# Feed-forward stages: each row product of 512 columns issued as two products of 256 columns

## What is computed

```
a = relu(h @ w1) ** 2        # w1: 1024 x 4096, a: 256 x 4096
x = x + gate * (a @ w2)      # w2: 4096 x 1024
```

## Time and profile before

| | us |
|---|---|
| Median of three executions | 1924.4 |
| Lowest and highest of them | 1923.17, 1924.47 |
| Span of the profiled execution, first to last instruction | 1914.2 |
| Median time minus that span | 10.2 |
| TensorE busy (share of span) | 1775.9 (93%) |
| VectorE busy | 779.1 (41%) |
| ScalarE busy | 490.0 (26%) |

### The profile page before, as it was taken

One profiled execution on the slowest core, in us unless ns is written; L12 is line 12 of the kernel. 1 busy time (PEld: TensorE's weight loads), 2 busy tenths in 40 slices (PEclk: granted clock), 3 DMA queues, 4 the chain that ended last, 5 costly groups with the idle time before them and its releaser, 6 DMA issues. The chain is left out here.

```text
span 1914.2 us, 23879 instructions
## 1 busy us (share of the span) xinstructions
PE 1775.9 (93%) x9783; PEld 1091.0 (57%) x9784; DVE 779.1 (41%) x1062; ACT 490.0 (26%) x593; POOL 72.3 (4%) x89
## 2 busy tenths in 40 slices
PE   6998889999999998999889898799899999989999
PEld 5873664333333333333323332598799977668898
DVE  5647661222112212212112121567754566666544
ACT  4334421001001000001000000443434453445442
POOL 7300000000000000000000000200000000000000
PEclk9999889999999999999999999899999999989999
DMA  8649799999999999999999999653365544775551
GB/s 291 219 136 385 264 421 398 427 428 428 427 427 427 428 427 427 428 427 427 428 428 427 428 427 419 226 193 124 133 220 176 176 147 163 266 262 178 193 182 63
DMA packets 133859, 598.28 MB, mean 313 GB/s; under 512 B 16897, under 2 KB 17041, under 8 KB 109057
## 3 DMA queue, kind: packets, MB, share of 16 engines
q1 hardware_dynamic: 126160, 589.34, 77.8%
q10 hardware_dynamic: 6800, 5.38, 1.0%
q0 software_dynamic: 800, 2.11, 0.3%
HBM read 595.70 MB, written 1.11 MB: 312 GB/s over the span
## 5 line engine op out<-in xcount | busy, mean ns | idle before, releaser
L175 DVE TENSOR_TENSOR wl<-raw,wh 128x2048 fp32r<-128x2048 f32 x126 | 289.5, 2328 | 85.4 <-ACT wh L169 85.3
L169 ACT ACTIVATE wh<-raw 128x2048 fp32r<-128x2048 f32 x126 | 236.6, 1912 | 171.0 <-PE banks L204 106.1
L1420 DVE COPY hid<-banks 128x512 f32<-128x512 f32 x32 | 22.1, 692 | 520.2 <-PE banks L1371 520.2
L233 PE MATMUL banks<-xth,wh 128*128 128x256 f32 x800 | 224.3, 280 | 8.0 <-DVE xtl L304 3.3
L233 PE MATMUL banks<-xtl,wh 128*128 128x256 f32 x800 | 223.4, 279 | 0.0
L233 PE MATMUL banks<-xth,wl 128*128 128x256 f32 x800 | 223.2, 279 | 0.0
L1371 PE MATMUL banks<-moe_halves,xs 128*64 128x512 f32 x816 | 187.4, 604 | 8.3 <-DMA moe_halves<-in_w_exp_in 8.3
L233 PEld LDWEIGHTS banks<-xth,wh 128*128 128x128 f32 x800 | 151.2, 189 | 9.6 <-DVE xtl L304 3.7
L233 PEld LDWEIGHTS banks<-xth,wl 128*128 128x128 f32 x800 | 151.3, 189 | 0.0
L233 PEld LDWEIGHTS banks<-xtl,wh 128*128 128x128 f32 x800 | 150.9, 189 | 0.3
L204 PE MATMUL banks<-wh,xth 128*128 128x512 f32 x320 | 128.8, 402 | 7.2 <-DVE wl L175 3.3
(11 more groups left out here) (409 smaller groups left out, 2250.4 us busy)
## 6 DMA issues: line engine op xcount, KB each, us to landing
moe_halves<-in_w_exp_in SPq DMA_DIRECT2D x51, 2048.0 KB, 40.9
raw<-in_mlp_w SPq DMA_DIRECT2D x64, 1024.0 KB, 5.6
moe_left<-in_w_exp_in SPq DMA_DIRECT2D x26, 2048.0 KB, 34.9
moe_halves<-in_w_exp_out SPq DMA_DIRECT2D x25, 2048.0 KB, 43.4
raw<-in_w_exp_in SPq DMA_DIRECT2D x25, 2048.0 KB, 40.0
raw<-in_ada_w SPq DMA_DIRECT2D x48, 1024.0 KB, 7.9
moe_left<-in_w_exp_out SPq DMA_DIRECT2D x14, 2048.0 KB, 43.1
moe_gates<-in_w_exp_in SPq DMA_DIRECT2D x13, 2048.0 KB, 38.7
```

The source lines that it names most:

```text
L169: act.activation(c.wh[:, slot], c.raw[:, slot], ACT.Copy).then_inc(c.high_ready, 1)
L175: dve.tensor_tensor(c.wl[:, slot], c.raw[:, slot], c.wh[:, slot].bitcast(F32), ALU.subtract).then_inc(c.low_ready, 1)
L233: mm = pe.matmul(out, w[:, slot, k, cols], x[:, k0 + k, :], start=first and k == 0 and j == 0 and b % 2 == 0, stop=last and k == CK - 1 an ...
L1420: dve.tensor_copy(c.hid[:, 1, :], c.bank[hid_banks(c, par) + 1]).then_inc(it.up_kept, 1)
```

## The change

A new function `multiply_halves` takes the place of `multiply_rows` in the feed-forward stages, for every row chunk but the last of the last quarter (which stays with `multiply_last`). Each product of 512 columns is issued as two of 256 columns, into the first and the second half of the same bank, with the same stationary operand, which the program loads again for the second half. The start flag is set for the first half alone.

```diff
+def multiply_halves(c, pe, n, slot, k0, banks, first, last, xh, xl):
+
+    pe.wait_ge(c.low_ready, n + 1)
+    for k in range(CK):
+        for m in range(len(banks)):
+            toks = slice(m * P, m * P + P)
+            for j, (x, w) in enumerate(((xh, c.wh), (xh, c.wl), (xl, c.wh))):
+                for b in range(2):
+                    cols = slice(b * COLS // 2, b * COLS // 2 + COLS // 2)
+                    mm = pe.matmul(banks[m][:, cols], x[:, k0 + k, toks], w[:, slot, k, cols],
+                                   start=first and k == 0 and j == 0 and b == 0, stop=last and k == CK - 1 and j == 2,
+                                   skip_group_check=True)
     mm.then_inc(c.used, 1)
...
                         else:
-                            multiply_rows(c, pe, i * QUARTER + (W + j), (W + j) % RING, h * CK,
-                                          (c.bank[p], c.bank[2 + p]), first and h == 0, False, ah, al, True)
+                            multiply_halves(c, pe, i * QUARTER + (W + j), (W + j) % RING, h * CK,
+                                            (c.bank[p], c.bank[2 + p]), first and h == 0, False, ah, al)
```

More of the change, by code:

```diff
@@ L206, in multiply_rows @@
                                skip_group_check=long)
+    mm.then_inc(c.used, 1)
+def multiply_halves(c, pe, n, slot, k0, banks, first, last, xh, xl):
[9 more added lines that the diff above has]
+                                   skip_group_check=True)
     mm.then_inc(c.used, 1)
```

## The result

Over 21 runs each, the changed kernel takes 1926.32 us in the median and the kernel before 1922.58; the ratio is 1.0016, 95% interval 1.0009 to 1.0023. That is 3.1 us more (1.7 to 4.4 by the interval; the medians themselves lie 3.7 us apart), a real but tiny loss inside of the 0.2% that I had named, where I had forecast 9.9 us less.

What follows compares the result with a forecast made beforehand. TensorE, busy without a break, was taken to bound both feed-forward stages. Row products 4.8 us and later columns 5.1 us less make 9.9 off 1924.4, forecasting 1914.5 us (own range 1912.8 to 1917; 8-in-10 range up to 1927.0).

Steps and rivals of the forecast that it cites:

- TensorE bounds the stages and nothing else is late: Both feed-forward stages: TensorE is busy throughout, its rate moves the end one for one, and no other engine loses the gain.
- The counts: Row products of both stages: 720 products of 512 columns become 1440 of 256, adding 720 matmuls and 720 loads.
- Rate of the row products: Halves in both stages keep quarter 0's fast column rate, 226.7 ns a pair against 233.3: 4.8 us less.
- Rate of the later columns: Column products of quarters 1 to 3, without 512-column products ahead, go from 117.8 to 113.35 ns: 5.1 us less.
- The rule of a fixed 2.5 ns: Skill page's gap per matmul, weighed against the trace: each pair 2.5 ns more, 1.8 us in all, giving 1926.2 us.
- Second load of the same operand: Row products: loading the same stationary tile again lies under a running product and costs nothing.
- more instructions: A quarter's row part: 192 matmuls and 192 loads in 22 us, the columns' density, cost nothing.
- the loop: Loop body grows from 288 products to 384; the jump back shows nothing today and was costed at nothing.
- The slow rate in the halves: Rival, chance 0.20: row products don't take over the columns' rate and lock at 117.8 ns; 1.6 us more, 1926.0 us.
- The third rate: Rival, chance 0.12: alternating halves settle into a slower period, priced at 120 ns; 7.3 us more, 1931.7 us.
- The range: Total time, 8 in 10: reaches over the differing stages and the slow rate to 1927.0 us, leaving out the third rate.
- The 10.2 us by which span and time were tied together: Whole execution: 10.2 us taken to lie around the profiled span of 1914.2 us when set against the runs' median.

Runs made afterwards that it cites:

- e8: Changed kernel with the row products' stationary operand taken from tiles xth and xtl instead of act_h and act_l; halves at 117.8 and 113.4 ns in turn, no time given.
- e1: Changed kernel with the two inner loops of multiply_halves swapped, so three products of one half follow each other; ratio to the kernel before 1.0015.
- e2: Changed kernel with stationary and moving operands swapped in the row products, weights stationary; 118.7 ns a product, no time given.
- e6: Changed kernel with only 64 of 128 stationary columns loaded in the row products; 116.7 ns a half, no time given.
- e7: Kernel before with only 64 of 128 stationary columns loaded for the 512-column row products; 229.4 or 231.1 ns each, no time given.
- e3: Kernel before with TensorE waiting for its own last row product ahead of the column products of quarters 1 to 3; ratio 1.0009.
- e5: Kernel before with two waits and eight plain float32 products ahead of the columns of quarters 1 to 3; 1935.45 us against 1921.35.
- e4: Changed kernel with each row product cut into four of 128 columns, each with its own weight load; 2078.18 us in one run.

## Why the prediction was wrong, point by point

- *TensorE bounds the stages and nothing else is late.* Right. The chain is TensorE alone in every run, also at 21.8 us a row piece.
- *The counts.* Right: 720 wide products became 1440 (three groups of 240 became three of 480).
- *Rate of the row products: fast, "since the halves of quarter 0 will come straight behind 192 column products that run at it, with the same width, and a rate once taken was held".* This step failed. I read a property of the operands' places as one of the stretch's past. Slots and row groups are multiples of 512 bytes apart, so that the relative place never changes within a stretch, which fits a rate that held for 480 products; I took this as proof that place doesn't matter. The halves have another relative place (128 in place of 192) and with it 118.7 ns. The term measured +2.9 us where I had -4.8. And the past of the stretch fails by itself: in the change, halves behind slow and behind fast columns take the same 22.78 and 22.79 us, and in e8, at the columns' own difference of 192, halves behind fast columns were slow.
- *Rate of the later columns: 5.1 us less.* Failed with it: 22.61 us, zero gained. I had 512-column products force the slow rate, and it doesn't take them: behind halves of 118.7, 117.8 or 120.0 ns the columns are slow as well. That halves can hand on the fast rate was right in e8 alone, at difference 192.
- *The rule of a fixed 2.5 ns.* The Trainium skill's page "TensorE: Matmul & The Clock Gate" (section "Back-to-back issue gap") would have the pairs at 1.8 us more in all; the page gives that formula for the gap of a single, isolated matmul. It came nearest to the measured 3.1, but the runs don't bear out its reason: at difference 0 a pair costs 13 ns more than the wide product, at 192, with the lower of the two values, 7 ns less.
- *Second load of the same operand, more instructions, the loop: nothing.* Right: swapping the order (e1) changed nothing, and pieces in and out of the loop are alike.
- *Rivals.* The slow rate in the halves (0.20) was right that the rate isn't handed on from columns to rows; it had the size roughly, 1.6 us for 2.9, and the wrong value, 117.8, and the roles of the operands, which it gave as the reason, don't matter (e2). The third rate (0.12) was right in "a period of their own" and wrong in its reason, the alternating halves: without them the rate is the same (e1). I had priced it from one interval of 120 ns, and 118.7 lay just under the 119.3 from which it decides (the prediction's 119.4 is a slip: 3.85 us over 720 pairs is 5.3 ns on 233.3). Nor did the columns take it over.
- *The range.* Its upper end of 1927.0 held the time, with some luck: the rivals that it was drawn over aren't what happened, and a loss of 3.1 us on the 1924.4 from which the prediction starts would be 1927.5; over 21 runs the kernel before has a lower median, 1922.58. The direction was wrong. The 10.2 us by which span and time were tied together drop out of the sum, which takes 9.9 off the time.

## What to carry to other kernels

Compare rates by the distance of starts, and before you carry a rate from one loop to another, compare where the operands lie, not just their shapes: here 64 to 384 bytes of padding moved fp32r products by up to 2.7%, with the other tile's place as the reference. A narrower product with its own load of 128 columns had little to gain here, since the narrowest one tried still took 111 ns; for 512-column fp32r products, the same start modulo 256 for stationary and moving tile is worth a try (227.0 against 233.3 ns here). Where the rest of the program scatters by 0.5%, a piece of the chain measures such an effect far better than the total.

## What the runs showed that I had not expected

- Two operands in on-chip memory set the rate of a matmul stream by their relative start modulo 256 bytes: 113.3 to 120.0 ns for 256 columns and 227.0 to 233.3 ns for 512, at granted clock 1.00 throughout. Narrow and wide products want different places: of those tried, 0 is the worst for the one and the best for the other. That it is a collision of the load's reads with the product's reads is a guess; shorter loads did change the rate (e6, e7), but no run shows the reads.
- At difference 192 the 256-column stream has two rates, and which one it takes changes from profile to profile. Over the 15 profiled executions in which the columns keep this place, quarter 0 was fast in 6 in the first stage and in 9 in the second, and the 480-product projection in 5, though none of the edits touches that projection or what comes before it. No kernel was profiled twice, so that two executions of one program differ in it is likely, not shown. Later quarters stayed slow but for one piece in e6 and those in e8. What picks between them is still open: neither a wait (e3) nor float32 products ahead (e5) brought the fast one, and the regular turns of slow and fast halves in e8, alike in both stages, speak against mere chance. These changes of rate alone move the time by up to 2.1 us in the projection (480 x 4.4 ns) and 0.85 us in each quarter 0.
- A product of 128 columns with its load took 111.5 ns (e4, at difference 128), where its columns take 53.3.
